# Asking for the first expert's rows while routing is still running, and four smaller reorderings, in a two-model stack on one Trainium2 core

## The reference, cut to what matters

```python
# first model, one of 2 layers; T = 16 + 512 tokens
proj = h @ w_in[li]                       # first 448 columns feed the MLA attention
...
h = _layer_norm(DN_ALPHA * h + mixed, ln1_g[li], ln1_b[li])
# _hier_moe: 4 groups x 8 experts, 2 experts a token
g_prob = softmax(h @ w_group + b_group)
e_logits = h @ w_expert + b_expert        # then the 8 of the token's group, top 2
xb = h[row_tok].reshape(n_blocks, BLOCK, D)
yb = (silu(xe @ w1[e]) * (xe @ w3[e])) @ w2[e]      # for every block of rows
y = zeros.at[row_tok].add(yb * row_gate)
# second model, third branch
cg = (h_lat @ w_in)[..., 3584:4096]       # the gate of the scan's output
```

## Time and profile before

| | us |
|---|---|
| median of 3 runs | 3777.72 |
| lowest and highest of them | 3768.35, 3783.77 |
| the profiled execution, its own time | 3792.31 |
| its span in the trace | 3790.1 |
| TensorE busy in it | 3228.9 (85%) |
| VectorE, ScalarE, GpSimd busy | 1686.6, 875.2, 371.8 |
| mean granted TensorE clock | 0.922 |

### The profile page before, as it was taken

One profiled execution on the slowest core, in us unless ns is written; L12 is line 12 of the kernel. 1 busy time (PEld: TensorE's weight loads), 2 busy tenths in 40 slices (PEclk: granted clock), 3 DMA queues, 4 the chain that ended last, 5 costly groups with the idle time before them and its releaser, 6 DMA issues. The chain is left out here.

```text
span 3790.1 us, 75666 instructions
## 1 busy us (share of the span) xinstructions
PE 3228.9 (85%) x32538; PEld 2387.0 (63%) x32538; DVE 1686.6 (45%) x3122; ACT 875.2 (23%) x1808; POOL 371.8 (10%) x530
## 2 busy tenths in 40 slices
PE   5899799985882899799985874889998989999998
PEld 0666599863441666699863442457656778878843
DVE  2244455533113344355542114435547776666611
ACT  3112322212113122222221113223344310022200
POOL 0000121001111000122001111000015400000000
PEclk7899799997996999799997896999999999999999
DMA  8211300208996110300208996110010023222221
GB/s 317 67 34 32 145 4 4 81 2 324 388 406 178 50 41 26 134 5 4 81 33 324 372 402 171 39 46 23 23 57 1 1 100 100 78 78 89 74 70 45
DMA packets 175277, 421.93 MB, mean 111 GB/s; under 512 B 25635, under 2 KB 122275, under 8 KB 146419
## 3 DMA queue, kind: packets, MB, share of 16 engines
q1 hardware_dynamic: 155987, 383.22, 27.5%
q0 software_dynamic: 8736, 17.32, 1.9%
q10 hardware_dynamic: 10240, 16.79, 1.3%
HBM read 400.55 MB, written 50.54 MB: 119 GB/s over the span
## 5 line engine op out<-in xcount | busy, mean ns | idle before, releaser
L2040 PE MATMUL ps<-e_w,e_xt 128*64 128x256 f32 x1792 | 230.5, 415 | 67.7 <-DMA e_w<-in_moe_w 66.1
L2040 PEld LDWEIGHTS ps<-e_w,e_xt 128*64 128x64 f32 x1792 | 151.4, 150 | 170.1 <-issue 84.1
L727 PE MATMUL ps<-h,win 128*128 128x264 f32 x960 | 233.6, 398 | 16.4 <-DVE pad L876 14.8
L2147 DVE TENSOR_TENSOR e_hid<-ps,e_silu 64x256 f32<-64x256 f32 x64 | 39.4, 616 | 416.6 <-ACT e_silu L2106 416.6
L727 PEld LDWEIGHTS ps<-h,win 128*128 128x128 f32 x960 | 181.1, 193 | 67.1 <-issue 38.2
L3530 PE MATMUL ps<-ff_up,wt 128*128 128x512 f32 x352 | 152.2, 592 | 0.0
L3470 PE MATMUL ps<-h_lat,wt 128*128 128x256 f32 x544 | 133.4, 388 | 15.1 <-DMA wt<-in_w_in 8.4
L1435 DVE COPY_PREDICATED inv<-level,ps 112x384 f32<-112x384 int32 x176 | 103.3, 587 | 86.4 <-PE ps L1336 78.2
L1336 PE MATMUL ps<-inv,nt 48*48 48x48 f32 x3520 | 131.1, 207 | 7.6 <-issue 6.4
L2059 PE MATMUL ps<-e_w,e_hid_t 128*64 128x512 f32 x448 | 115.5, 636 | 20.8 <-DMA e_w<-in_moe_w 17.1
L3470 PE MATMUL ps<-h_lat,w_sums 128*128 128x256 f32 x544 | 130.0, 382 | 0.0
(11 more groups left out here) (613 smaller groups left out, 6960.5 us busy)
## 6 DMA issues: line engine op xcount, KB each, us to landing
e_w<-in_moe_w SPq DMA_DIRECT2D x168, 1024.0 KB
wmod<-in_w_mod SPq DMA_DIRECT2D x24, 1024.0 KB, 13.8
early<-in_moe_w SPq DMA_DIRECT2D x24, 1024.0 KB, 15.0
wt<-in_w_up SPq DMA_DIRECT2D x22, 1024.0 KB, 5.0
y_rows<-e_y ACTq DMA_DIRECT2D x128, 128.0 KB
win<-in_w_in SPq DMA_DIRECT2D x10, 1536.0 KB, 6.6
wt<-in_w_in SPq DMA_DIRECT2D x12, 1024.0 KB, 6.1
wt<-in_w_down SPq DMA_DIRECT2D x16, 704.0 KB, 4.7
```

Of the source, the lines that this page charges most:

```text
L727: last = pe.matmul(ps[:, 7, 0:HT], lhsT=ring[(s + 1) % 2][:, i, o:o + P], rhs=k.h[:, i, h * HT:(h + 1) * HT], start=(i == 0), stop=(i == K ...
L2040: last = pe.matmul(ps[half, 2 + z, 0:EH], lhsT=xt[z][:, f, :], rhs=w[:, f, :], start=(f == 0), stop=(f == KD - 1))
L2147: dve.tensor_tensor(hid[z][high, :].rearrange("s (t q) -> s q t", t=2), ps[high, 2 + z, 0:EH].rearrange("s (q t) -> s q t", t=2), si[z][hi ...
```

## The change

It has five parts. (1) The gather of the first slot's rows is issued by GpSimd in routing, from `first_idx`, one column of the table that DVE takes out as soon as it is made; the buffer `first_x` is blanked there too. In routing the six row stores are issued between the early experts' loads and not behind them: expert 1, rows 0 to 2, expert 2, rows 3 to 5, expert 3. (2) In `experts`, SP waits for that gather before it requests the ring's first weights. (3) The router's two halves go to partitions 0 to 35 and 64 to 99 of one PSUM bank, and the transposes and copies behind them follow. (4) The first projection waits for half of its weights, adds blocks 0 to 3 of all eight results, and then blocks 4 to 7. (5) The gate's first 128 columns are requested at the end of `branch_attention`, into a tile of their own.

```diff
@@ mix_in
-                sp.dma_start(ring[0][:, :, 0:MLA_COLS], w[:, :, 0:MLA_COLS]).then_inc(win_mla, 16)
-                sp.dma_start(ring[0][:, :, MLA_COLS:512], w[:, :, MLA_COLS - ROPE:MLA_COLS]).then_inc(win_mla, 16)
+                for i, landed in ((0, win_mla), (KD // 2, win_rest)):
+                    of = slice(i, i + KD // 2)
+                    sp.dma_start(ring[0][:, of, 0:MLA_COLS], w[:, of, 0:MLA_COLS]).then_inc(landed, 16)
+                    sp.dma_start(ring[0][:, of, MLA_COLS:512], w[:, of, MLA_COLS - ROPE:MLA_COLS]).then_inc(landed, 16)
...
-                pe.wait_ge(win_mla, 32)
-                for m in range(4):
-                    for h in range(2):
-                        for i in range(KD):
-                            last = pe.matmul(ps[:, 2 * m + h, 0:HT], lhsT=ring[0][:, i, m * P:(m + 1) * P],
-                                             rhs=k.h[:, i, h * HT:(h + 1) * HT], start=(i == 0), stop=(i == KD - 1))
-                    last.then_inc(lat_made, 1)
+                for part in range(2):
+                    pe.wait_ge((win_mla, win_rest)[part], 32)
+                    for m in range(4):
+                        for h in range(2):
+                            for i in range(part * KD // 2, (part + 1) * KD // 2):
+                                last = pe.matmul(ps[:, 2 * m + h, 0:HT], lhsT=ring[0][:, i, m * P:(m + 1) * P],
+                                                 rhs=k.h[:, i, h * HT:(h + 1) * HT], start=(i == 0), stop=(i == KD - 1))
+                        if part:
+                            last.then_inc(lat_made, 1)
@@ mix_close
-                        last = pe.matmul(ps[0:NR, 2 + h, 0:HT], lhsT=k.router[:, f, :],
+                        last = pe.matmul(ps[N_B * h:N_B * h + NR, 2, 0:HT], lhsT=k.router[:, f, :],
...
-                dve.tensor_scalar(split2(k.logits_t[:, :]), ps[0:NR, 2:4, 0:HT], k.router_b[:, 0:1], None,
-                                  ALU.add).then_inc(logits_kept, 1)
+                for b in (0, N_B):
+                    dve.tensor_scalar(k.logits_t[b:b + NR, :], ps[b:b + NR, 2, 0:HT], k.router_b[b:b + NR, 0:1], None,
+                                      ALU.add).then_inc(logits_kept, 1)
@@ route
-            for n in range(SOON, PRE):
-                load_early(k, a, li, sp, n)
+            load_early(k, a, li, sp, SOON)
             for j in range(NC1):
                 sp.wait_ge(kept, j + 1)
                 sp.dma_start(k.h_rows[j * TC:(j + 1) * TC, :], rows[:, j, :]).then_inc(stored, 16)
+                if j == 2:
+                    load_early(k, a, li, sp, SOON + 1)
+            for n in range(SOON + 2, PRE):
+                load_early(k, a, li, sp, n)
             sp.wait_ge(stored, 16 * NC1)
...
             gpo.memset(slots[:, NBLK:NBLK + 1], 0).then_inc(tail_set, 1)
+            gpo.memset(first_x[:, :], 0.0).then_inc(tail_set, 1)
+            gpo.wait_ge(tail_set, 2)
+            gpo.wait_ge(stored, 16 * NC1)
+            gpo.wait_ge(first_idx_set, 1)
+            gpo.indirect_dma_start(
+                out=first_x[:, :], out_offset=None, in_=k.h_rows[:, :],
+                in_offset=bass.IndirectOffsetOnAxis(ap=first_idx[:, 0:1].bitcast(U32), axis=0),
+                bounds_check=T - 1, oob_is_err=False).then_inc(k.pool_sems["x_in0"], 16)
...
             chain(dve.tensor_scalar(owner[:, :], ownf[:, :], float(EXPERTS - 1), None, ALU.min))
+            dve.wait_ge(listed, 1)
+            dve.tensor_scalar(first_idx[:, :], ps[0:SLOT, 6, 0:1], float(ROWS), None, ALU.add).then_inc(first_idx_set, 1)
...
-            dve.wait_ge(listed, 1)
             chain(dve.tensor_scalar(slots[:, 0:NBLK], ps[0:SLOT, 6, 0:NBLK], float(ROWS), None, ALU.add))
@@ experts
-    x = [sb(f"e_x{z}", [SLOT, D]) for z in Z]
+    x = [first_x, sb("e_x1", [SLOT, D])]
...
+            sp.wait_ge(x_in[0], 16)
             for n in range(AHEAD):
                 load_up(n % 2, owner[0:1, n:n + 1], freed(n))
...
-            for z in Z:
-                gp.memset(x[z][:, :], 0.0).then_inc(blank_set, 1)
-            gp.wait_ge(blank_set, 2)
-            for s in range(S0 + 1):
+            gp.memset(x[1][:, :], 0.0).then_inc(blank_set, 1)
+            gp.wait_ge(blank_set, 1)
+            for s in range(1, S0 + 1):
@@ branch_attention
+            sp.dma_start(gate_w[:, :, :], w_in[:, :, 3584:3584 + P]).then_inc(gate_w_in, 16)
             sp.wait_ge(lb_out, 32)
@@ gated_scan
-    g = [sb(f"c_gm{z}", [P, 8, P]) for z in D2]
+    g = [gate_w, sb("c_gm1", [P, 8, P])]
...
-            for m in range(2):
-                sp.dma_start(ring[m][:, :, :], w_in[:, :, 3584 + m * P:3584 + (m + 1) * P]).then_inc(wcg_in[m], 16)
+            sp.dma_start(ring[1][:, :, :], w_in[:, :, 3584 + P:3584 + 2 * P]).then_inc(wcg_in[1], 16)
...
             for m in range(4):
-                pe.wait_ge(wcg_in[m % 2], 16 * (m // 2 + 1))
+                if m == 0:
+                    pe.wait_ge(gate_w_in, 16)
+                else:
+                    pe.wait_ge(wcg_in[m % 2], 16 * ((m + 1) // 2))
```

More of the change, by code:

```diff
@@ L660, in two @@
             return ps[:, 2 * (t % 3):2 * (t % 3) + 2, 0:HT]
-        with k.stage("par_in", "uq_in", "win_mla", "win_odd", "win_even", "rest_in", "lat_made", "lat_kept", "squared",
+        with k.stage("par_in", "uq_in", "win_mla", "win_rest", "win_odd", "win_even", "rest_in", "lat_made", "lat_kept", "squared",
                      "summed", "root", "normed_in", "slot_made", "dve_emptied", "act_emptied", "filled", "emptied",
@@ L1694, in moe @@
         pairs = sb("pairs", [1, 1], I32)
+        first_x, first_idx = sb("first_x", [SLOT, D]), sb("first_idx", [SLOT, 1], I32)
         k.early += [early_place(k, n) for n in range(SOON, PRE)]
         with ExitStack() as rt:
-            route(k, a, li, rt, gate, dest, slots, owner, pairs)
+            route(k, a, li, rt, gate, dest, slots, owner, pairs, first_x, first_idx)
         with ExitStack() as ex:
-            experts(k, a, li, ex, slots, owner, pairs, k.early, k.early_in)
+            experts(k, a, li, ex, slots, owner, pairs, k.early, k.early_in, first_x)
         with ExitStack() as cb:
@@ L1702, in moe, with route @@
         k.right.close()
-def route(k, a, li, rt, gate, dest, slots, owner, turns_left):
+def route(k, a, li, rt, gate, dest, slots, owner, turns_left, first_x, first_idx):
     nc, ps = k.nc, k.ps
@@ L1763, in _ @@
             for j in range(NC1):
[L1764 to L1765 removed]
+                of = slice(N_B * (2 * j // NC1), N_B * (2 * j // NC1) + NR)
+                at = j % (NC1 // 2) * TC
+                last = pe.transpose(ps[0:TC, 6 + 2 * j // NC1, j % 3 * NR:(j % 3 + 1) * NR],
+                                    k.logits_t[of, at:at + TC], k.ident[of, of])
             last.then_inc(made, 1)
@@ L1907, in _, with experts @@
             chain(dve.tensor_copy(turns_left[:, :], ownf[:, 0:1]))
-            dve.wait_ge(listed, 1)
             chain(dve.tensor_scalar(slots[:, 0:NBLK], ps[0:SLOT, 6, 0:NBLK], float(ROWS), None, ALU.add))
-def experts(k, a, li, ex, slots, owner, turns_left, early, early_in):
+def experts(k, a, li, ex, slots, owner, turns_left, early, early_in, first_x):
     nc, ps = k.nc, k.ps
@@ L2308, in second_block @@
                     right.close()
-                    branch_attention(k, a, at, w_in, hl, hc, q, kt, v, ys, cq, lf, cv)
+                    gate_w = k.sb("gate_w", [P, KD, P], stack=right, side="right")
+                    gate_w_in = right.enter_context(nc.semaphore("gate_w_in"))
+                    branch_attention(k, a, at, w_in, hl, hc, q, kt, v, ys, cq, lf, cv, gate_w, gate_w_in)
                 with ExitStack() as t:
                     gated_scan(k, a, t, w_in, hl, cq, lf, cv, ys[2],
-                               hc[:, :, :].rearrange("p (h b) n -> p h (b n)", h=4))
+                               hc[:, :, :].rearrange("p (h b) n -> p h (b n)", h=4), gate_w, gate_w_in)
+                right.close()
             with ExitStack() as tl:
@@ L2566, in attend, with branch_attention @@
     return q, kt, v
-def branch_attention(k, a, at, w_in, hl, hc, q, kt, v, ys, cq, lf, cv):
+def branch_attention(k, a, at, w_in, hl, hc, q, kt, v, ys, cq, lf, cv, gate_w, gate_w_in):
     nc, ps = k.nc, k.ps
@@ L2930, in gated_scan @@
                  "moved", "out_kept",
-                 "pool_chain", "scan_chain") as (
+                 "pool_chain", "scan_chain", also=[gate_w_in]) as (
             block, spans_in, bound_in, wcg_in0, wcg_in1, gate_made, gate_kept, q_ready, prepared, limited,
```

26 lines of the change are left out of this document (13 added, 13 removed).

## The result

| | before | after |
|---|---|---|
| median, us | 3777.38 (4 runs) | 3744.65 (4 runs, 3742.37 to 3746.76) |
| ratio | 1 | 0.9912, 95% interval 0.9895 to 0.9928 |
| profiled execution, its span | 3792.31, 3790.1 | 3746.76, 3744.8 |
| mean granted TensorE clock | 0.922 | 0.926 |

The kernel is 32.7 us faster. The two profiled executions differ by 45.6 us, because the one of before lies 15 above its median.

The account below looks back on a forecast made before the run. DMA engines loading the experts' weight ring were taken as the limit, with TensorE idle for the late gather. 18.0 + 7.0 + 7.2 + 5.0 = 37.2 us off the 3777.72 median gave 3740.5, range 3726 to 3761.

Parts of the forecast that it names:

- The likeliest case: Whole kernel: the forecast with its ends, gains of 25 to 48 us; chance 0.74.
- rival E: Routing's end: it waits for GpSimd's DMA, harmless since PE needs the landing anyway; 3742 us, chance 0.03.
- the stage's end: Routing closes with GpSimd's gather issue at about 880.6; the next stage opens at about 882, ahead of the landing.
- SP's first ring load later than before: Experts' start: a named sign of being wrong; the forecast had this load at 887.4 instead of 887.87.
- the hole: Between the ring's first loads and SP's next request, DMA share 0.25; closing it gains 6.4 us, 6.8 in layer 1.
- the 1.6 I had counted: Experts' later 143 us stretch, engines waiting for PE: up to 3 us recoverable, within the step from 7.4 to 9.0.
- The second gather: Experts, GpSimd: issued at about 884, there by 893.3 when needed; if late, nothing lost until 2 us.
- Rival A: Experts: the ring's first loads set the end, parts 1 and 2 bring 0.5 to 1 a layer; 3756, within 0.10.
- B: Router: the column halves don't overlap, so 7.0 us fall out of the sum; 3747.5 us, chance 0.08.
- C: Whole kernel: two parts fail together, say the hole stays and the halved load waits; 3764 us, chance 0.12.
- D: Experts' start: gather lands late in both layers, gains used up at 905, 3784 us at 908; chance 0.04.
- my two values for the clock: Head of `gated_scan`: granted clock falls to 0.50 as before, or stays up and gains 2.3 us more.

Follow-up runs that it names:

- The two repeats: The changed kernel unaltered, compared twice more with the kernel before: 3752.12 us (ratio 0.9932) and 3757.83 us (ratio 0.9921).
- the 4 and 6 kernels: Profiled kernels without parts 1 and 2 (4), and with stores between the loads and gather in routing (6); routing to `combine`, layer 0: 318.4 and 312.2 us.
- only_gather: Kernel before with only the gather in routing, reordered row stores and held ring: 3767.21 us, ratio 0.9964.
- after_again: The changed kernel once more, unaltered, on another chip: 3752.12 us, ratio 0.9932 to the kernel before.
- only_router: Kernel before with only the router's two halves in two column halves of the array: 3773.95 us, ratio 0.9983.
- the four single runs: Each alone on the kernel before: gather with hold, ratio 0.9964; router 0.9983; first projection 0.9974; gate weights 0.9994.
- the three kernels in which the clock fell to 0.8: only_gate and both late_gather kernels; the gate's first tile took 8.80 us, the stretch around it 542.4 us on average.
- late_gather: Changed kernel with the gather as GpSimd's first instruction in `experts` and no hold: 3747.31 us, ratio 0.9926; repeated, 3752.38 us, 0.9897.
- only_gate: Kernel before with only the gate's first 128 columns requested in the stage ahead: 3775.95 us, ratio 0.9994.

## Why the prediction was right, and where it wasn't

- **Forecast** 3740.5 us, 37.2 gained; measured 3744.65, 32.7 gained. The two repeats, 28.3 and 31.7, say that the sum was some 4 to 9 us too high. The likeliest case held, with rival E inside it.
- **What bounds it**: right. The wait for ring weights stayed (67.7, then 68.3), the idle time before the first rows went.
- **Parts 1 and 2**, 18.0 forecast: 15.2 by the stretches, 11.6 to 13.6 alone. The step that failed is the stage's end. I let it close with GpSimd's issue and open the next 1.4 us later. It stays open until the gather has landed, 5.84 us after its issue, then the boundary takes its 1.6, and SP needs another 1.06. So the ring's first load came not 0.5 us sooner but 1.15 and 2.4 later (means over the 4 and 6 kernels: 36.99 to 38.14, 35.53 to 37.94). That is 2.3 a layer less. The prediction had named this as a sign of being wrong ("SP's first ring load later than before"), and it showed. If the hole closed as worked out (6.4 and 6.8), the rest gave 0.9 a layer more than the 1.6 I had counted: 9.0 - 2.3 + 0.9 = 7.6, which is 15.2 in two layers. The 0.9 is only what is left over, and smaller than the error of the stretches.
- **Gather's timing**: index and stores as forecast (28.5 and 27.7 us after routing's start against 27.8 and 27.2), and so was the landing, 35.4 against 35.5, by the packets. PE was 1.7 us later than the 35.5, for the boundary again. The early expert's product took 5.59 us for the 5.03 forecast, and SP's next request went out at 51.75 where I had 48.6. The 3.67 us that I took for the first ring product held in this profile, but not in only_gather and after_again (6.32 and 6.23). The second gather, which I had on time, was 1.96 us late; I had put the bound at which that costs anything at 2, and DMA share stayed at 1.01.
- **How queues share**: I read from the earlier trace rows that a gather doesn't stand behind what another queue has requested. The rows don't show it. Three loads of the ring, 3 MB, had been requested before the gather at 889.87, and at 408 GB/s they can be through by its landing; the two others were requested behind it. No term of the sum rested on it.
- **The hold**: worth 0.5 as I had it, nothing as measured. My reason for it, that the next stage opens ahead of the landing, was false.
- **Rival E** came true: a stage end that waits for GpSimd's DMA. I gave it 0.03 and a time of 3742, and called it harmless; it cost the 2.3 us a layer above. The trace of before had the pattern at hand: routing stayed open until SP's stores had landed. I read that as the explicit wait of SP and didn't ask whether GpSimd's queue would be held for its own DMA.
- **Rival A** fell: the experts' stretch got 6 to 9 us shorter, not 0.5 to 1. **B** fell with only_router, **C** with the four single runs, **D** with the landing at 35.4 us after routing's start.
- **Router**, 7.0 forecast, 6.8 by the stretches and 6.4 alone. I had PE at the low clock as what sets the time, 6.6 us for its group; that is what only_router shows (6.63), while in the changed kernel ACT sets it (5.67).
- **First projection**, 7.2 forecast, 5.8 by the stretches. Two terms were mis-sized. I took layer 1's gap of 9.15 us for both layers, and layer 0's is 8.70. And the start-up that doesn't shrink with the bytes, 2 us in my sum, comes out of the same formula as 2.4 us in layer 0 (2 x 5.54 - 8.70) and 4.0 in layer 1 (2 x 6.73 - 9.41).
- **Gate**, 5.0 forecast, 5.3 measured. The 4.0 us of idle time went as forecast. Of my two values for the clock the better one came true in the changed kernel (1.00 throughout), 2.3 us, and 0.7 of it went to the third weight tile, since only the first had been loaded ahead. But the three kernels in which the clock fell to 0.8 have the same stretch of 542.4 us: their `gated_scan` is 1.2 us longer, and the stage ahead of it as much shorter. So that the clock's part counts in the total isn't shown, and the good sum owes something to luck.

## What to carry to other kernels

A gather moved into an earlier stage moves that stage's end to its landing: count the landing, not the issue, and ask what else starts at that boundary. Where a ring of weights feeds an engine, its first release matters as much as its first load; 7 us won at the front were mostly lost to the hole that came back. And a latency read from a row with other traffic, and with more rows to move, is no lower bound for a small transfer alone.

## What the runs showed of the hardware

- A stage with an indirect DMA of GpSimd as its last instruction stays open until the rows have landed. The next stage opened 4.06 us after the issue with the DMA engines at a share of 0.08, and 7.45 us after it with the last early weights moving, both times 1.6 us behind the last packet of GpSimd's queue; without the gather it opened 30.6 us after routing's start in place of 37.0.
- The first rows' gather took about 7.5 us from issue to PE's use beside 5 MB of ring loads (late_gather, 869.57 to 877.03), the same as the 8.0 before.
- Two matmuls on the same rows and different column ranges, 36 wide, run side by side: 0.21 us a record at a clock of 0.56, 0.44 alone at 0.50.
- TensorE, idle for 3.09 us where it had been idle for 7.08, kept a granted clock of 1.00 at the head of `gated_scan`, and its first tile took 7.11 us. In only_gate, after 3.10 us of idle time, the clock was 0.81 over 6 us and the tile took 8.80; both late_gather kernels did the same after 3.09 and 3.10. What decides between the two stays open.
